# Gated units' up projections as seven products of halves instead of eight, with the norm's scale on the rows

## What is computed

```python
def conv_ffn(xn, w_up, conv_w, conv_b, w_down):
    val, gate = jnp.split(xn @ w_up, 2, axis=-1)        # w_up: 1024 x 5632
    gp = jnp.pad(gate, ((0, 0), (CONV_W - 1, 0), (0, 0)))
    gc = conv_b + conv_w[0] * gp[:, 0:seq]
    for j in range(1, CONV_W):
        gc = gc + conv_w[j] * gp[:, j:j + seq]
    return (jax.nn.silu(gc) * val) @ w_down             # w_down: 2816 x 1024
...
    h = h + conv_ffn(rms_norm_2(h, ffn_norm[layer]), ffn_w_up[layer], ...)
```

## Time and profile before

| | us |
|---|---|
| median of 3 runs (2288.08 to 2289.93) | 2288.26 |
| span of the profiled execution, first to last instruction | 2287.9 |
| TensorE busy | 2236.4 (98%) |
| VectorE busy | 1255.1 (55%) |
| ScalarE busy | 990.6 (43%) |
| GpSimd busy | 360.9 (16%) |
| mean granted clock of TensorE | 0.993 of full |

### The profile page before, as it was taken

The page is one execution under the profiler, slowest core; times in us unless marked ns, Lnnn a source line. Parts: engine busy times, 40 slices in busy tenths (PEclk is TensorE's granted clock), DMA queues, the critical chain, the costliest instruction groups (busy, mean ns, idle before and its releaser), DMA issues.

```text
span 2287.9 us, 30159 instructions
## 1 busy us (share of the span) xinstructions
PE 2236.4 (98%) x11479; PEld 1806.6 (79%) x11479; DVE 1255.1 (55%) x2250; ACT 990.6 (43%) x1835; POOL 360.9 (16%) x432
## 2 busy tenths in 40 slices
PE   7899999999999999999989999999999999999999
PEld 6677777788877787878878888888888668888887
DVE  6966565756645454544493555464444565454543
ACT  7445655533554545463432423333344664232322
POOL 7742131126202030300000000000034000000000
PEclk9999999999999999999999999999999999999999
DMA  7354212134232222225462232322222302322232
GB/s 224 118 170 129 74 56 93 43 105 157 101 112 68 87 80 87 86 71 176 164 213 89 78 111 79 106 92 85 100 92 92 130 20 74 111 92 93 93 101 83
DMA packets 184559, 236.70 MB, mean 103 GB/s; under 512 B 29565, under 2 KB 110932, under 8 KB 184418
## 3 DMA queue, kind: packets, MB, share of 16 engines
q1 hardware_dynamic: 160462, 207.73, 28.1%
q10 hardware_dynamic: 23956, 27.04, 3.7%
HBM read 215.84 MB, written 23.10 MB: 104 GB/s over the span
## 4 chain that ended last, share of the span: by engine, by line
PE 88%; DVE 7%; ACT 2%; issue 1%; POOL 1%; DMA 1%; SPq 0%; ACTq 0%; DVEq 0%; POOLq 0%
PE G L2211 25%; PE G L2213 25%; PE G L2212 25%; DVE w_lo L1762 1%; PE X L2220 1%; PE X L2331 1%; PE X L2342 1%; PE X L2319 1%; PE X L2358 1%; PE X L2345 1%; PE G L2365 1%; PE G L2379 1%; PE X L2315 1%; PE X L2230 1%; POOL small L1172 1%
## 5 line engine op out<-in xcount | busy, mean ns | idle before, releaser
L2211 PE MATMUL G<-w_hi,u_hi 128*128 128x512 f32 x1536 | 622.5, 405 | 4.0 <-issue 2.1
L2213 PE MATMUL G<-w_hi,u_lo 128*128 128x512 f32 x1536 | 601.2, 391 | 0.0
L2212 PE MATMUL G<-w_lo,u_hi 128*128 128x512 f32 x1536 | 599.8, 391 | 0.0
L1762 DVE SCALAR_TENSOR_TENSOR w_lo<-raw,par,w_hi 128x512 fp32r<-128x512 f32 x496 | 373.6, 791 | 402.5 <-ACT w_hi L1250 399.6
L1250 ACT ACTIVATE w_hi<-raw,par 128x512 fp32r<-128x512 f32 x496 | 318.2, 714 | 342.3 <-PE G L2213 339.2
L2211 PE MATMUL G<-u_hi,w_hi 128*128 128x512 f32 (+1 forms) x1168 | 458.2, 392 | 0.3 <-DVE w_lo L1762 0.2
L2213 PE MATMUL G<-u_hi,w_lo 128*128 128x512 f32 (+1 forms) x1168 | 446.0, 382 | 0.0
L2212 PE MATMUL G<-u_lo,w_hi 128*128 128x512 f32 (+1 forms) x1168 | 445.8, 382 | 0.0
L2211 PEld LDWEIGHTS G<-w_hi,u_hi 128*128 128x128 f32 x1536 | 289.1, 188 | 70.1 <-issue 8.7
L2213 PEld LDWEIGHTS G<-w_hi,u_lo 128*128 128x128 f32 x1536 | 288.8, 188 | 62.3
L2212 PEld LDWEIGHTS G<-w_lo,u_hi 128*128 128x128 f32 x1536 | 289.5, 188 | 59.2 <-issue 1.9
(11 more groups left out here) (315 smaller groups left out, 2334.4 us busy)
## 6 DMA issues: line engine op xcount, KB each, us to landing
raw<-in_ffn_w_up SPq DMA_DIRECT2D x88, 512.0 KB, 4.7
raw<-in_e_w_in SPq DMA_DIRECT2D x56, 512.0 KB, 4.7
raw<-in_o_w_in SPq DMA_DIRECT2D x56, 512.0 KB, 4.5
raw<-in_ffn_w_down SPq DMA_DIRECT2D x40, 512.0 KB, 4.3
raw<-in_e_w_out SPq DMA_DIRECT2D x16, 512.0 KB, 4.6
raw<-in_o_w_out SPq DMA_DIRECT2D x16, 512.0 KB, 4.2
raw<-in_a_w_glu SPq DMA_DIRECT2D x16, 512.0 KB, 4.9
raw<-in_w_kv SPq DMA_DIRECT2D x16, 512.0 KB, 4.7
```

Source lines behind the costliest of these rows:

```text
L1762: V.scalar_tensor_tensor(w_lo[:, n % HL, k], raw[:, n % RAW, k], gain(name, k0 + k), w_hi[:, n % HL, k].bitcast(F32), ALU.mult, ALU.subtract)\
L2211: pe.matmul(out, lh, rh, start=start, stop=False)
L2212: pe.matmul(out, lh, rl, start=False, stop=False)
L2213: return pe.matmul(out, ll, rh, start=False, stop=stop)
```

## The change

The first chunk of each up projection stays as it was. The other ten go through a new stage, `seven`. For it the tokens are halved (256 and 256), the features are halved (512 and 512), and the 512 columns of a chunk are halved in gate and value, so that a chunk is a product of two matrices of two by two pieces. Strassen's scheme, in Winograd's form, makes it of seven products instead of eight, from sums of pieces:

- Of the tokens, four sums S1 to S4, once for each up projection. GpSimd makes them (`pool_token_sums`) in eight instructions of 1024 columns: four join high and low part again, four add or subtract. ScalarE and VectorE split them again (`token_high`, `token_low`). S1 takes the place of a piece of `u_hi` and `u_lo` that is no longer needed, the other three lie in `su_hi` and `su_lo`.
- Of the weights, four sums T1 to T4 in each chunk, made by GpSimd from `raw` into `att` (`pool_weight_sums`, one instruction of 1024 columns each, the second and third on the result of the one before).
- Seven products in each chunk, each two blocks of twelve matmuls over 256 tokens: 168 in a chunk. For each, ScalarE makes 1024 columns of `w_hi` in one instruction (`product_high`) and VectorE 1024 of `w_lo` (`product_low`), in a ring of four half buffers. ScalarE runs three products ahead of TensorE, VectorE two.
- The products' sums: part of them is made in PSUM by leaving a bank's sum standing for the next product, part on the way out. ScalarE copies four intermediate results of 512 columns to SBUF, VectorE adds four times PSUM to SBUF (c11, c12, c21, c22).
- The gate now comes to SBUF (`work`) first, and the convolution reads it there, still in three instructions for each of the two row tiles. SiLU and the product with the value become one instruction of 1024 columns each, in the next chunk.
- `raw` of the next chunk may be loaded when T3 is made and B11 or B22 is split.

The norm's gain no longer goes on the weights: `unit_gain` of these units is None, so the first chunk's units take L1246's and L1757's form. It goes on the token rows with the inverse root, in one instruction with two SBUF operands (`rms_tiles`), from `row_scale`, which is loaded for all partitions by a DMA of 512 KB once for each up projection.

The core of the diff:

```diff
+SEVEN = 10
+PRODUCTS = (("A11", "B11"), ("A12", "B21"), ("S1", "T1"), ("S2", "T2"), ("S4", "B22"), ("A22", "T4"), ("S3", "T3"))
...
-                gains.append((f"ffn{layer}", k0))
+                gains.append(None)
...
+        def ring(s, q):
+            return (s.first + q // 2) % 2, slice(256 * (q % 2), 256 * (q % 2) + 256)
+        A_HALF = {"A11": (slice(0, 4), slice(0, 256)), "A12": (slice(4, 8), slice(0, 256)),
+                  "A22": (slice(4, 8), slice(256, 512)), "S1": (slice(0, 4), slice(256, 512))}
+        SU = {"S2": 0, "S3": 1, "S4": 2}
+        RAW_HALF = {"B11": (0, 0), "B12": (0, 256), "B21": (1, 0), "B22": (1, 256)}
+        MADE = {"T1": 0, "T2": 1, "T3": 2, "T4": 3}
...
+                    if n - RAW in seven:
+                        s = seven[n - RAW]
+                        j, u = divmod(n - RAW - s.n, 2)
+                        sp.wait_ge(*at_("sw_done", s.i, 7 * j + 4 * u))
+                        sp.wait_ge(*at_("sw_made", s.i, j, "T3"))
...
+                pool.wait_ge(*at_("u_ready", s.norm.i, TT - 1, 1))
+                join("A21")
+                join("A22")
+                made("S1", of["A21"], of["A22"], ALU.add)
+                join("A11")
+                made("S2", token_sum("S1"), of["A11"], ALU.subtract)
+                join("A12")
+                made("S4", of["A12"], token_sum("S2"), ALU.subtract)
+                made("S3", of["A11"], of["A21"], ALU.subtract)
+            def pool_weight_sums(s, j):
+                B = {name: weight_half(s, j, name) for name in (*RAW_HALF, *MADE)}
+                def made(name, a, b):
+                    if j:
+                        q = 7 * (j - 1) + [x[1] for x in PRODUCTS].index(name)
+                        pool.wait_ge(*at_("sw_done", s.i, q))
+                    pool.tensor_tensor(B[name], B[a], B[b], ALU.subtract).then_inc(*by("sw_made", s.i, j, name))
+                for u in range(2):
+                    n = s.n + 2 * j + u
+                    pool.wait_ge(raw_loaded[n % RAW], 32 * (n // RAW + 1))
+                    if u == 0:
+                        made("T1", "B12", "B11")
+                pool.wait_ge(*at_("sw_made", s.i, j, "T1"))
+                made("T2", "B22", "T1")
+                pool.wait_ge(*at_("sw_made", s.i, j, "T2"))
+                made("T4", "B21", "T2")
+                made("T3", "B22", "B12")
...
+            def product_high(s, q):
+                if q >= 7 * SEVEN:
+                    return
+                j, p = divmod(q, 7)
+                name = PRODUCTS[p][1]
+                if name in MADE:
+                    act.wait_ge(*at_("sw_made", s.i, j, name))
+                else:
+                    n = s.n + 2 * j + RAW_HALF[name][0]
+                    act.wait_ge(raw_loaded[n % RAW], 32 * (n // RAW + 1))
+                act.wait_ge(blocks, s.base + q - 3 if q >= 4 else bb[s.n - 2] + 4 * (q // 2) + 4)
+                r, c = ring(s, q)
+                nc.scalar.activation(w_hi[:, r, :, c], weight_half(s, j, name), ACT.Copy)\
+                    .then_inc(*by("sw_high", s.i, q))
+            def seven_silu(s, j):
+                act.wait_ge(*at_("s_conv", s.i, j, 1))
+                nc.scalar.activation(conv_rows(j), conv_rows(j), ACT.Silu).then_inc(*by("s_act", s.i, j))
+            def act_seven(s):
+                for q in range(7 * SEVEN):
+                    j, p = divmod(q, 7)
+                    product_high(s, q + 3)
+                    if q == 0:
+                        token_high(s, "S3")
+                    if p == 1:
+                        act.wait_ge(blocks, product_at(s, j, 0))
+                        if j >= 2:
+                            act.wait_ge(*at_("s_conv", s.i, j - 2, 1))
+                        nc.scalar.activation(gate_rows(j)[:, :, 0:256], chain_bank(j), ACT.Copy)\
+                            .then_inc(*by("p1", s.i, j))
+                    if p == 3:
+                        act.wait_ge(blocks, product_at(s, j, 2))
+                        nc.scalar.activation(value_rows_of(j)[:, :, 256:512], two(G[:, 2, :]), ACT.Copy)\
+                            .then_inc(*by("p5", s.i, j))
+                    if p == 4:
+                        act.wait_ge(blocks, product_at(s, j, 3))
+                        nc.scalar.activation(value_rows_of(j)[:, :, 0:256], chain_bank(j), ACT.Copy)\
+                            .then_inc(*by("u2", s.i, j))
+                    if p == 6:
+                        act.wait_ge(blocks, product_at(s, j, 5))
+                        nc.scalar.activation(gate_rows(j)[:, :, 256:512], two(X[:, s.aux[j] % 4, :]), ACT.Copy)\
+                            .then_inc(*by("p4", s.i, j))
+                    if p == 4 and j:
+                        seven_silu(s, j - 1)
+                    if j == SEVEN - 1 and p == 4:
+                        act.wait_ge(*at_(*s.ahead.first_y))
+                        y_split(s.ahead, 0)
...
+                    if s.rows is not None:
+                        dve.wait_ge(rows_loaded, 16 * (s.rows + 1))
+                        V.scalar_tensor_tensor(xn_view[:, t, :], h[:, t, :], rstd[:, t:t + 1], row_scale,
+                                               ALU.mult, ALU.mult).then_inc(*by("xn_ready", s.i, t))
+                        continue
...
+            def product_low(s, q):
+                if q >= 7 * SEVEN:
+                    return
+                j, p = divmod(q, 7)
+                r, c = ring(s, q)
+                dve.wait_ge(*at_("sw_high", s.i, q))
+                V.tensor_tensor(w_lo[:, r, :, c], weight_half(s, j, PRODUCTS[p][1]), w_hi[:, r, :, c].bitcast(F32),
+                                ALU.subtract).then_inc(*by("sw_done", s.i, q))
+            def seven_conv(s, j, m):
+                c = 2 * (j + 1) + m
+                dve.wait_ge(*at_("c21", s.i, j))
+                conv(conv_rows(j)[:, m, :], gate_rows(j)[:, m, :], lambda i: gain(f"f{s.layer}_cw{i}", c),
+                     gain(f"f{s.layer}_cb", c)).then_inc(*by("s_conv", s.i, j, m))
+            def seven_y(s, j):
+                y = value_rows_of(j)
+                dve.wait_ge(*at_("s_act", s.i, j))
+                V.tensor_tensor(y, y, conv_rows(j), ALU.mult).then_inc(*by("s_y", s.i, j))
+            def seven_late_half(s, j):
+                value, gate = value_rows_of(j)[:, :, 256:512], gate_rows(j)[:, :, 256:512]
+                dve.wait_ge(blocks, product_at(s, j, 6))
+                dve.wait_ge(*at_("p4", s.i, j))
+                V.tensor_tensor(gate, chain_bank(j), gate, ALU.add).then_inc(*by("c21", s.i, j))
+                V.tensor_tensor(value, chain_bank(j), value, ALU.add).then_inc(*by("c22", s.i, j))
+            def dve_seven(s):
+                for q in range(7 * SEVEN):
+                    j, p = divmod(q, 7)
+                    product_low(s, q + 2)
+                    if q == 0:
+                        token_low(s, "S3")
+                    if j and p == 0:
+                        seven_late_half(s, j - 1)
+                    if j and p in (1, 3):
+                        seven_conv(s, j - 1, p // 2)
+                    if p == 2:
+                        dve.wait_ge(blocks, product_at(s, j, 1))
+                        dve.wait_ge(*at_("p1", s.i, j))
+                        gate = gate_rows(j)[:, :, 0:256]
+                        V.tensor_tensor(gate, two(G[:, 3, :]), gate, ALU.add)\
+                            .then_inc(*by("c11", s.i, j))
+                    if j and p == 4:
+                        seven_y(s, j - 1)
+                    if p == 5:
+                        dve.wait_ge(blocks, product_at(s, j, 4))
+                        dve.wait_ge(*at_("u2", s.i, j))
+                        value = value_rows_of(j)[:, :, 0:256]
+                        V.tensor_tensor(value, two(G[:, 2, :]), value, ALU.add).then_inc(*by("c12", s.i, j))
+                    if j == SEVEN - 1 and p == 5:
+                        y_rest(s.ahead, 0)
...
+            def pe_seven(s):
+                for q in range(7 * SEVEN):
+                    j, p = divmod(q, 7)
+                    a, _ = PRODUCTS[p]
+                    r, c = ring(s, q)
+                    pe.wait_ge(*at_("sw_done", s.i, q))
+                    if j == 0 and a[0] == "S":
+                        pe.wait_ge(*at_("su_done", s.i, a))
+                    if p == 0:
+                        pe.wait_ge(*(at_("c22", s.i, j - 2) if j >= 2 else at_(*gfreed[j][s.c - 1])))
+                    elif p == 1:
+                        pe.wait_ge(*(at_("c11", s.i, j - 1) if j else at_(*gfreed[3][s.c - 1])))
+                    elif p == 2:
+                        pe.wait_ge(*(at_("c12", s.i, j - 1) if j else at_(*gfreed[2][s.c - 1])))
+                    elif p == 3:
+                        pe.wait_ge(*at_("p1", s.i, j))
+                    elif p == 4:
+                        pe.wait_ge(*at_("p5", s.i, j))
+                    elif p == 6:
+                        pe.wait_ge(*at_("u2", s.i, j))
```

(9 more changed lines are left out.)

249 lines of the change are left out of this document (196 added, 53 removed).

## The result

The changed kernel takes 2342.49 us (median of 4 runs, 2340.97 to 2347.15) against 2289.1 us (2288.08 to 2291.05): the ratio is 1.0237, 95% interval 1.0225 to 1.025. The change costs 53 us, where 11 were forecast, and the range ended at 2312. The direction was right and the size was not.

What follows compares the result with a forecast made beforehand. TensorE bound the kernel before; VectorE, held by GpSimd's sums, would bound the new stage. Per projection 1.5 (chunks) + 1.5 (start) + 2 (end) + 0.5 (norm) = 5.5, both 11: 2288.3 + 11 = 2299 us, range 2258 to 2312.

Steps and rivals of the forecast that it cites:

- 17.5 more for its ten chunks: Ten chunks of an up projection: 219.1 us in all, with 20.5 for the first, 22.2 for eight, 21.0 for the last.
- TensorE, 0.227 to 0.120 us a matmul, 20.16 us a chunk: TensorE in a chunk: 168 half-width matmuls at 120.0 ns take 20.16 us, where the chunk took 21.76.
- The ceiling of 16.0 us in a projection: Most that TensorE's saving can win if it stays the bound: 1.60 us in each of 20 chunks, 32.0 us.
- VectorE's own work, 15.5: VectorE's instructions in a chunk, without GpSimd's holds, sum to 15.5 us, under TensorE's 20.16.
- A GpSimd sum, 1.79 less the overlap of 0.5 a chunk: Each GpSimd weight sum costs VectorE 1.79 us, four 7.15 a chunk, less 0.5 overlap: a chunk of 22.2.
- the upper bound of 23.0: VectorE's chunk at worst, 23.0 us, if each GpSimd sum costs it 1.87.
- Start of the stage, 1.5: Token sums through to the third product delay each projection's stage by zero to 2 us, taken as 1.5.
- End of the stage, 2: Last chunk: VectorE's work ahead of the down projection's first w_lo costs 0 to 4 us, taken as 2.
- Norm, 0.5: Gain on the token rows and single-piece w_hi cost -0.5 to 1.5 us a projection, taken as 0.5.
- ScalarE and the loads hidden: In a chunk, ScalarE's 10.8 us and the raw loads with sums, 14.3 to 19.0 us, cost nothing.
- The rival had matmuls slower in the gaps: TensorE's half-width matmuls run slower than 120 ns or the clock falls in gaps: 2295 to 2310 us, chance 0.03.
- The rival built on it: Ports held for GpSimd's whole instruction, or late loads: chunks of 23.3 to 24 us, 2312 to 2325; 0.08 above 2312.

Runs made afterwards that it cites:

- e3: Changed kernel with GpSimd's weight sums and token sums both cut to 4 columns, the rest of these sums left out: 2271.0 us, ratio 0.9923.
- e1: Changed kernel with GpSimd's four weight sums in each chunk cut to 4 columns instead of 1024, token sums kept: 2289.7 us, ratio 1.0003.
- e7: Kernel before with only the norm's part of the change, the gain on the token rows instead of the weights: 2289.3 us, ratio 1.0003.
- e2: Changed kernel with GpSimd's eight token-sum instructions cut to 4 columns, weight sums kept: 2319.2 us, ratio 1.0136.
- e9: Kernel before with four useless GpSimd sums of 1024 columns added to each of chunks 2 to 10: 2287.6 us, ratio 0.9994.
- e11: Kernel before with eight useless GpSimd sums of 1024 columns added to each of chunks 2 to 10: 2304.5 us, ratio 1.0066.
- e6: Changed kernel with weight sums on VectorE, new queue order, GpSimd's token sums later, convolution's first instruction on ScalarE: 2276.8 us, ratio 0.9945.
- e8: Changed kernel with each GpSimd weight sum of 1024 columns made as two instructions of 512: 2322.5 us, ratio 1.0140.
- e12: Changed kernel with weight sums on VectorE, GpSimd's token sums later, another start order, convolution whole on VectorE: 2282.3 us, ratio 0.9969.
- e13: Changed kernel with weight and token sums all on VectorE, convolution whole on VectorE, queues reordered at the start: 2280.5 us, ratio 0.9968.

## Why the prediction was right in direction and wrong in size

The mechanism was the one forecast: VectorE, held by GpSimd's sums, becomes the bound. What failed is the size of two terms of the sum: the start of the stage, put at 1.5 us a projection, which took 18 and 16 in the two, and the price of a GpSimd sum, put at 1.66 us, which is 1.85. The start is read on TensorE: from the norm's last split to the first chunk's sixth product (the one that goes to `X`) it lasts 50.4 and 48.2 us, where e3 has 38.5 and 37.7 with some 6 us of its own loss in them (above), so 12 and 10 more than e3 and 18 and 16 in all. The nine distances from sixth product to sixth product last 203.5 and 206.2 us, 22.1 and 24.7 more than 9 x 20.16; the forecast had 17.5 more for its ten chunks. So of the 40 us by which the two stages missed the forecast, some 30 came at the start and 12 in the chunks, and the end took 2 less than its term.

- **TensorE, 0.227 to 0.120 us a matmul, 20.16 us a chunk: right.** e1 shows 20.16 for chunk after chunk. The ceiling of 16.0 us in a projection held, but only 9.6 and 10.4 of it arrived even with every sum all but gone (e3), since the step took for granted that the first chunk's end would not stand in the way.
- **VectorE's own work, 15.5: nearly.** 15.84 by e1.
- **A GpSimd sum, 1.79 less the overlap of 0.5 a chunk, so 1.66 net: too small.** Where a sum meets an instruction of 1024 columns, that one takes 3.36 us instead of 1.22, 2.14 more. The earlier trace rows had a sum against pieces of 512, and I scaled it by GpSimd's columns alone. More lay under the additions out of PSUM than I gave it (12 of the 32 in eight chunks), so that the net price is 1.85, 7.4 us a chunk for 6.65. With 0.3 more of own work and 0.2 of idle time VectorE's period is 23.4 (pairs of 46.8) and not 22.2, over the upper bound of 23.0. For eight full chunks that would be 10 us in a projection; on TensorE, which begins the chunks two products ahead, 5 and 7 arrived. The three misses are small and of one sign, and the bound took single figures as exact.
- **Start of the stage, 1.5: wrong, the term most mis-sized (18 and 16).** The token sums alone cost 9 to 11 us (e1 against e3), and the multiplication behind the splits 6 (e3). The prediction followed one chain, GpSimd's sums to the third product, and priced GpSimd's pace in it. It did not ask what VectorE had to do in the same 20 us: four `w_lo` pieces (10.39 for 2.49) and the first product's `w_lo` (3.38), both beside sums, and convolution and multiplication queued behind them. It did not follow what the late pieces hold up in turn, the load of `raw` and with it the second product's `w_hi` and S1's split. And it did not look at what stood on VectorE's queue ahead of the multiplication that frees the second product's bank. The rows for it were there (the earlier trace rows has exactly four pieces stretched from 2.49 to 7.93).
- **End of the stage, 2: too large.** TensorE has one wait of 0.7 us there, and from the last sixth product to the down projection's first addition to `h` it is 64.1 and 64.0 us, for 63.0 in e3.
- **Norm, 0.5: too small to be measured.** e7 is at 1.0003; the wait of 0.8 us is there in e7 too.
- **ScalarE and the loads hidden: right in the chunks.** GpSimd waits for the loads, 188 us in both stages, and gives the moment at which three sums start in a row; but in the chunks from 1345 to 1560 us ScalarE waited for a load at most 0.8 us. At the start it waited 11 (above).
- **The clock.** The rival had matmuls slower in the gaps, at 0.03. It was seen: behind the stall of 3.5 us shown above the matmuls are 0.21 apart for 6 us (27 of them take 1432.28 - 1426.38 = 5.9 us, 2.7 more than at 0.12). That is the longest such stretch of the trace: behind the five waits of 3.5 us in the two stages stood between 2 and 26 distances of that kind. Added up over a stage, and at its start over matmuls of 512 columns too, the slow distances make some 11 us by the trace. They do not add to the time where VectorE sets the period, since VectorE is busy 99% of it all the same; they do where TensorE is the bound, 2.3 us in e3.

By causes, first and second projection: won on TensorE -9.6 and -10.4 (e3 against before, with the wait for the bank in it), weight sums +24.1 and +27.3, token sums +11.0 and +8.8; sum +25.5 and +25.8. (Taken in the other order, by e2, the token sums are +11.3 and +11.4, so the split between the two is good to 3 us.) The forecast had -16, +17.5 with the stage's two end chunks in it, and 4 for start, end and norm. The Trainium skill ("SBUF — State Buffer", Who interferes with whom) has whoever starts first hold the ports for its whole instruction; by the trace a VectorE instruction that meets a sum takes 2.14 us longer, of GpSimd's 2.44, so for a single meeting this reading was nearer than mine, while the average over a chunk is 1.85. The rival built on it, 23.3 to 24 us a chunk and 2312 to 2325, had the chunks' period (23.4 on VectorE) and missed the start as the forecast did.

## What to carry to other kernels

Work that is put on GpSimd because it is idle isn't free when VectorE is the next engine in line: hold VectorE's own time plus what each sum takes from it against the period of the bound. For a sum of 1024 columns that was 1.85 us here (2.14 where it surely meets an instruction of 1024 columns), and 1.2 and 1.4 in e9 and e11, where VectorE's pieces are of 512 and many read PSUM. If that passes the period, put the work on VectorE itself, where the same sum costs 1.14. Do that sum for the first and the last microseconds of a stage too, and read there which instruction frees the first bank and what is queued ahead of it. Where estimates lie within a few per cent of the turning point and all small omissions have one sign, the range must reach past the "worst" sum.

## What the runs showed of the hardware

- **Turns between GpSimd and VectorE.** In e6, two GpSimd sums of 1024 columns that find VectorE idle when they start take 4.88 us, 2.44 each (the line below); in a row of turns with VectorE's 1024 columns (1.22 alone) each of both takes 3.35:

```profile
1306.06 4.88 POOL L1300 TENSOR_TENSOR big<-u_hi,u_lo 128x1024 f32<-128x1024 f32 x2 [7.82 <-DVE w_lo L1995]
```

- **Smaller instructions cost less in sum.** The same columns in two instructions took 1.59 us from VectorE instead of 1.85, the waits were even and short, and the granted clock in the chunks stayed at 1.00: 20 us for splitting one instruction (e8).
- **A stall costs more than itself, but not always the same.** After waits of 3.5 and 3.9 us TensorE ran with half-width matmuls 0.21 apart for 0.12 over 5 to 6 us, at a granted clock of 0.50, the lower of its two levels (1.2 and 2.4 GHz). Other waits of 3.5 us in the same trace left as few as two such distances. Two waits of 1.71 and 1.84 us with three matmuls between them, at the start of the stage, were enough too: the next ones of 512 columns are 0.43 apart for 0.227, at 0.50 from 1316.3 to 1319.3. Waits of 1.3 us (e8), one to a chunk of 22.3, did not lower the granted clock that the window shows.
- **Full engines side by side.** With VectorE at 99% (e12, e13) TensorE kept its 20.16 us a chunk in the first projection and 20.2 in the second. VectorE's additions come 20.27 apart in e12, so it falls behind by 0.1 us a chunk, and that is paid at the end: the stage's last part is 64.3 us for 63.0 in e3.
